# First head of a retention block: forward scan before the query sum, which goes in halves

## The reference

```
q = rotary(q); k = rotary(k) * Dh**-0.5           # x*cos + swapped(x)*sin
scores = (q_chunk @ k_chunk.T) * decay_in         # inside a chunk
inner  = scores @ v
chunk_kv = (k * zeta).T @ v                       # state that a chunk adds
state  = chunk_decay * state + chunk_kv           # scan over the 16 chunks
cross  = (q * xi) @ state_before_the_chunk
y = inner + cross     # once forward, once backward, summed, then normed and gated
```

## Time and profile before

| | us |
|---|---|
| median of 3 runs | 2922.72 |
| lowest and highest | 2922.49, 2923.69 |
| the profiled execution | 2928.47 |
| its span, first to last instruction | 2926.4 |
| TensorE busy | 2803.2 (96%) |
| VectorE busy | 1371.2 (47%) |
| GpSimd busy | 879.6 (30%) |
| ScalarE busy | 576.0 (20%) |

### The profile page before, as it was taken

The page is one execution under the profiler, slowest core; times in us unless marked ns, Lnnn a source line. Parts: engine busy times, 40 slices in busy tenths (PEclk is TensorE's granted clock), DMA queues, the critical chain, the costliest instruction groups (busy, mean ns, idle before and its releaser), DMA issues.

```text
span 2926.4 us, 37167 instructions
## 1 busy us (share of the span) xinstructions
PE 2803.2 (96%) x13882; PEld 2357.4 (81%) x13882; DVE 1371.2 (47%) x1527; ACT 576.0 (20%) x1060; POOL 879.6 (30%) x439
## 2 busy tenths in 40 slices
PE   5899999998989999999999999999999999999998
PEld 4788888887767898888888888778988888888887
DVE  4593939486875333522414234433345224152343
ACT  5221212213544222100001001232221000010012
POOL 1242423344962000333333333220003333333331
PEclk8999999999999999999999999999999999999999
DMA  4133333326853222111111113132221111111111
GB/s 159 47 116 122 105 118 118 122 99 226 257 187 115 94 83 76 51 43 50 46 47 50 46 48 108 58 122 94 87 72 51 43 50 50 43 50 50 43 50 72
DMA packets 289754, 253.99 MB, mean 87 GB/s; under 512 B 8016, under 2 KB 253960, under 8 KB 283400
## 3 DMA queue, kind: packets, MB, share of 16 engines
q1 hardware_dynamic: 266320, 203.45, 22.3%
q10 hardware_dynamic: 23352, 49.39, 4.7%
HBM read 196.71 MB, written 56.10 MB: 86 GB/s over the span
## 4 chain that ended last, share of the span: by engine, by line
PE 81%; DVE 11%; issue 3%; DMA 2%; ACT 2%; POOL 1%; ACTq 0%; DVEq 0%; SPq 0%; POOLq 0%
PE ps L699 23%; PE ps L694 23%; PE ps L695 23%; DVE acc L1685 6%; PE ps L1038 2%; PE ps L1040 2%; PE ps L1039 2%; DVE st_f L1765 1%; DMA wb<-wqk_d 1%; DVE alo L1951 1%; PE ps L1000 0%; PE ps L1049 0%; PE ps L885 0%; DVE alo L1819 0%; DMA out<-rows 0%
## 5 line engine op out<-in xcount | busy, mean ns | idle before, releaser
L554 POOL TENSOR_SCALAR whi<-wraw 128x1024 fp32r<-128x1024 f32 x192 | 224.9, 1171 | 1920.1 <-PE ps L699 1189.9
L694 PE MATMUL ps<-ahi,whi 128*128 128x512 f32 x1376 | 543.0, 395 | 17.7 <-DVE alo L1951 11.5
L695 PE MATMUL ps<-alo,whi 128*128 128x512 f32 x1376 | 538.5, 391 | 0.0
L556 POOL TENSOR_TENSOR wlo<-wraw,whi 128x1024 fp32r<-128x1024 f32 x192 | 522.8, 2723 | 16.0
L694 PE MATMUL ps<-bhi,whi 128*128 128x512 f32 x1024 | 399.4, 390 | 2.3 <-DVE blo L1872 2.3
L695 PE MATMUL ps<-blo,whi 128*128 128x512 f32 x1024 | 398.4, 389 | 0.0
L1685 DVE SCALAR_TENSOR_TENSOR acc<-upad,taps,acc 128x2048 f32<-128x2048 f32 x120 | 347.8, 2898 | 15.7 <-DVE acc L1682 0.6
L699 PE MATMUL ps<-ahi,wlo 128*128 128x512 f32 x1376 | 340.1, 389 | 0.0
L694 PE MATMUL ps<-xhi,whi 128*128 128x512 f32 x768 | 305.8, 398 | 20.9 <-DVE xlo L1607 11.0
L694 PEld LDWEIGHTS ps<-ahi,whi 128*128 128x128 f32 x1376 | 259.9, 189 | 78.6 <-DVE alo L1951 14.9
L1523 ACT ACTIVATE ahi<-z 128x512 f32 x128 | 80.9, 632 | 1140.9 <-DVE z L1948 1140.9
(11 more groups left out here) (260 smaller groups left out, 3668.8 us busy)
## 6 DMA issues: line engine op xcount, KB each, us to landing
wraw<-in_w_ff SPq DMA_DIRECT2D x128, 512.0 KB, 3.7
proj_d<-st ACTq DMA_DIRECT2D x64, 256.0 KB, 2.5
wraw<-in_w_in SPq DMA_DIRECT2D x24, 512.0 KB, 4.5
xt<-in_x SPq DMA_DIRECT2D x16, 512.0 KB, 6.4
wraw<-in_w_xkv SPq DMA_DIRECT2D x16, 512.0 KB, 5.2
vwo_d<-pst ACTq DMA_DIRECT2D x16, 512.0 KB, 3.6
wqk_d<-pst ACTq DMA_DIRECT2D x16, 512.0 KB, 3.6
wraw<-in_w_out SPq DMA_DIRECT2D x16, 512.0 KB, 4.7
```

Source lines behind the costliest of these rows:

```text
L554: pool.tensor_scalar(whi[:, slot, :, :], wraw[:, slot, :, :], 1.0, 0.0, ALU.mult, ALU.add).then_inc(w_hi, 1)
L556: pool.tensor_tensor(wlo[:, slot, :, :], wraw[:, slot, :, :], whi[:, slot, :, :], ALU.subtract).then_inc(w_ready, 1)
L694: nc.tensor.matmul(o, whi[:, slot, k, :], hi(k), start=(k == order[0]), stop=False)
L695: nc.tensor.matmul(o, whi[:, slot, k, :], lo(k), start=False, stop=False)
```

## The change

In the first head alone, VectorE runs the forward scan right behind the straight query, and the query sum behind the scan. The sum is made in two halves of 1024 tokens, the later half first, each with a signal on a new semaphore `q_rot_up`; the old one, `q_rot`, is raised when both are done. TensorE's scores wait per quarter for the half that they read. GpSimd's decayed queries of the first head are made in eight instructions of 512 tokens in place of two of 2048, quarter by quarter in the order in which `retained` reads them, and `retained` waits for its own quarter (`decays_done`). The later heads keep their instructions; their waits on `p_qf` are renumbered, since the first head now raises it eight times.

```diff
--- before.py
+++ after.py
@@ -234,6 +234,11 @@
         pre_st = [sem("pre_st0"), sem("pre_st1")]

         G0 = 4
+
+        def decays_done(h, j=3):
+
+            return 2 * j + 2 if h == 0 else 8 + 2 * h
+
         DEC_LIN = 10 + HEADS
         DEC_EXP = 2 + 4 * HEADS

@@ -274,7 +279,7 @@
         dec_in, iot, dec_dve, dec_act = (sem(n) for n in ("dec_in", "iot", "dec_dve", "dec_act"))
         l_sin, l_cos, dpos, dlin, zero_st = sem("l_sin"), sem("l_cos"), sem("dpos"), sem("dlin"), sem("zero_st")
         p_qs, p_ks, p_qc, p_kc, p_qf = sem("p_qs"), sem("p_ks"), sem("p_qc"), sem("p_kc"), sem("p_qf")
-        r_q, r_k, q_rot, k_rot = sem("r_q"), sem("r_k"), sem("q_rotd"), sem("k_rotd")
+        r_q, r_k, q_rot, k_rot, q_rot_up = sem("r_q"), sem("r_k"), sem("q_rotd"), sem("k_rotd"), sem("q_rot_up")
         kt_mm, vt_mm, kt_ev, vt_ev = sem("kt_mm"), sem("vt_mm"), sem("kt_ev"), sem("vt_ev")
         v2, v_sum, v_cen = sem("v2"), sem("v_sum"), sem("v_cen")
         kvf_mm, kvb_mm, f_scan, b_scan = sem("kvf_mm"), sem("kvb_mm"), sem("f_scan"), sem("b_scan")
@@ -610,14 +615,20 @@
                 pool.tensor_tensor(qb_[:, :], qb_[:, :], cos_t[:, :], ALU.mult).then_inc(p_qc, 1)

             def decayed_q(h):
-                pool.wait_ge(q_rot, h + 1)
+                if h:
+                    pool.wait_ge(q_rot, h + 1)
                 pool.wait_ge(dec_act, DEC_EXP + 2 * h + 2)
                 if h:
                     pool.wait_ge(y_mm, 4 * h)
-                for dst, xi in ((q_f, xi_f), (q_b, xi_b)):
-                    pool.tensor_tensor(dst[:, :].rearrange("p (c q) -> p c q", q=P),
-                                       q_rot_b[:, :].rearrange("p (c q) -> p c q", q=P),
-                                       xi[:, bass.ds(h, 1), :].to_broadcast([P, CH, P]), ALU.mult).then_inc(p_qf, 1)
+                for part in DOWN if h == 0 else (None,):
+                    at = slice(0, S) if part is None else slice(part * NC, (part + 1) * NC)
+                    chunks = (at.stop - at.start) // P
+                    for dst, xi in ((q_f, xi_f), (q_b, xi_b)):
+                        if part is not None:
+                            pool.wait_ge(q_rot_up, 1 if part >= 2 else 2)
+                        pool.tensor_tensor(dst[:, at].rearrange("p (c q) -> p c q", q=P),
+                                           q_rot_b[:, at].rearrange("p (c q) -> p c q", q=P),
+                                           xi[:, bass.ds(h, 1), :].to_broadcast([P, chunks, P]), ALU.mult).then_inc(p_qf, 1)

             def gated(h):
                 for j, i in enumerate(TURNS[h]):
@@ -877,9 +888,12 @@
                     last.then_inc(kvb_mm, 1)

             def scores_in(h):
-                pe.wait_ge(q_rot, h + 1)
+                if h:
+                    pe.wait_ge(q_rot, h + 1)
                 pe.wait_ge(f_scan, 15 * h + 15)
                 for i in DOWN:
+                    if h == 0:
+                        pe.wait_ge(q_rot_up, 1 if i >= 2 else 2)
                     for c in range(4):
                         cc = 4 * i + c
                         last = pe.matmul(ps[:, i, c * P:(c + 1) * P], k_rot_b[:, cc * P:(cc + 1) * P],
@@ -889,7 +903,7 @@
             def retained(h, j):

                 i = DOWN[j]
-                pe.wait_ge(p_qf, 2 * h + 2)
+                pe.wait_ge(p_qf, decays_done(h, j))
                 pe.wait_ge(s_ev, 4 * h + j + 1)
                 pe.wait_ge(b_scan, 15 * h + min(4 * j + 4, 15))
                 for c in range(4):
@@ -1742,15 +1756,23 @@
                 dve.wait_ge(p_ks, h + 1)
                 dve.tensor_tensor(k_rot_b[:, :], kb_[:, :], ksb[:, :], ALU.add).then_inc(k_rot, 1)

+            def straight_q0():
+                dve.wait_ge(l_q, 16)
+                dve.wait_ge(l_cos, 16)
+                dve.tensor_tensor(qb_[:, :], qb_[:, :], cos_t[:, :], ALU.mult).then_inc(r_q, 1)
+
+            def rotate_q0():
+                dve.wait_ge(r_q, 1)
+                dve.wait_ge(p_qs, 1)
+                for half in range(2):
+                    at = slice((1 - half) * HALF, (2 - half) * HALF)
+                    dve.tensor_tensor(q_rot_b[:, at], qb_[:, at], qsb[:, at], ALU.add).then_inc(q_rot_up, 1)
+                dve.wait_ge(q_rot_up, 2)
+                dve.sem_inc(q_rot, 1)
+
             def rotate_q(h):
-                if h == 0:
-                    dve.wait_ge(l_q, 16)
-                    dve.wait_ge(l_cos, 16)
-                    dve.tensor_tensor(qb_[:, :], qb_[:, :], cos_t[:, :], ALU.mult).then_inc(r_q, 1)
-                    dve.wait_ge(r_q, 1)
-                else:
-                    dve.wait_ge(p_qc, h)
-                    dve.wait_ge(p_qf, 2 * h)
+                dve.wait_ge(p_qc, h)
+                dve.wait_ge(p_qf, decays_done(h - 1))
                 dve.wait_ge(p_qs, h + 1)
                 dve.tensor_tensor(q_rot_b[:, :], qb_[:, :], qsb[:, :], ALU.add).then_inc(q_rot, 1)

@@ -1821,13 +1843,15 @@
             rotate_k(0)
             dve.memset(st_f[:, 0, :], 0.0).then_inc(zero_st, 1)
             dve.memset(st_b[:, CH - 1, :], 0.0).then_inc(zero_st, 1)
-            rotate_q(0)
+            straight_q0()
             dve.wait_ge(dec_act, DEC_EXP)
             dve.wait_ge(zero_st, 2)

             for h in range(HEADS):
                 last = h + 1 == HEADS
                 forward_scan(h)
+                if h == 0:
+                    rotate_q0()
                 for j in range(4):
                     backward_scan(h, j)
                     masked_scores(h, j)
```

## The result

The changed kernel takes 2927.58 us (median of 20 runs, 2925.58 to 2934.32), beside 2923.2 us for the kernel before in the same rounds (20 runs). The ratio is 1.0017, with a 95% interval of 1.0010 to 1.0024: some 5 us slower, at the edge of what was called no change (5.8 us). In later rounds the ratio was 1.0009 (0.9999 to 1.0018), some 2.6 us, so the size of the loss is known only roughly. The profiled execution had a span of 2926.0 us and took 2927.95 us, less than the one of before, because its first phase happened to end 3.4 us earlier. So a whole span tells nothing here, and one distance is used from now on, the *head measure*: from the start of the first head's swapped query on GpSimd to the start of head 1's forward scan on VectorE. It is 766.59 - 717.81 = 48.78 us before.

What follows compares the result with a forecast made beforehand. TensorE holds 81% of the chain, but the first head's end hangs on GpSimd's list through `k_rot`. Delay +1.9 and clock +1.5 make +3.4 us: 2922.72 + 3.4 = 2926.1 us, range 2921.5 to 2929.

Steps and rivals of the forecast that it cites:

- Where the end hangs: End of the first head: `k_rot` of head 1, behind GpSimd's list, comes last, some 0.55 us later than TensorE's path.
- The query sum later: First head, VectorE: the query sum, now behind the scan, is ready later and delays GpSimd by 1.0 us.
- The quarters: First head, GpSimd: eight decay instructions in place of two long ones cost 0.9 to 1.0 us more.
- the lock: VectorE and GpSimd share ports, held by whoever starts first; without it the first decay quarter would start 1.1 us earlier.
- The clock: Tail before head 1's scan: TensorE's clock falls in an 8.8 us pause, costing 0.7 to 2.2 us, taken as 1.5.
- The sum: Whole kernel: +1.9 us of delay and +1.5 us of clock make +3.4 us; head 1's scan near 770.
- TensorE's path decides: Handover to head 1: the tail starts when `retained` ends, 8.5 us earlier, giving 2914.2 us; rival, 5%.
- `k_rot` gets ahead of `q_in`: Handover to head 1: VectorE has the port first, `k_rot` ends 2.3 us early, 2920.4 to 2922 us; rival, 8%.
- A low clock through the next scores: Head 1's states and scores: the clock is not back when they begin, about +9 us, 2932 us; rival, 5%.
- no clock cost: Tail before head 1's scan: only GpSimd's delay counts, +1.0 to +2.7 us, 2924.6 us; rival, 17%.
- the change does what it says: First head: scores start near 724.7, 6.0 us earlier; the rival, no start before 730, gives +1 to +2 us, 3%.

Runs made afterwards that it cites:

- e4: The changed kernel, with GpSimd starting head 1's straight query only when head 1's `k_rot` is done; ratio 1.0005 (0.9995 to 1.0014).
- e6: The changed kernel with e4's wait and head 1's straight key moved from GpSimd to VectorE; 2922.45 us, ratio 0.9988 (0.9979 to 0.9997).
- e8: The changed kernel with 72 unused identity turns on TensorE between the first head's last `retained` and head 1's key turns; ratio 1.0009 (0.9998 to 1.0021).
- e7: e6 with the wait for the next head's `k_rot` in each of the first three heads; 2921.47 us, ratio 0.9988 (0.9978 to 0.9998).
- e9: The kernel before, with only e4's wait, put into each of the first three heads; ratio 0.9997 (0.9988 to 1.0006).
- e3: The changed kernel with 56 unused identity turns on TensorE, in the same place as the 72 of e8; ratio 1.0011 (1.0001 to 1.0022).

## Why the prediction was right, and where its terms were off

- **Where the end hangs.** `k_rot` of head 1, behind GpSimd's list, was named as the last wait; the new chain says the same, e4 and e6 move the handover through it, and the second profile of the kernel before keeps its measure while TensorE is 0.5 us earlier.
- **The query sum later: 1.0 us forecast, 0.3 measured** against the swapped query in this profile. The mis-sized step is the start of the scan: it was worked out from chunk states at the low clock (5.45 us), and they ran at the full one (3.81). Which clock they get differs from one execution to the next (3.81 to 5.99 us for the same 32 records in the 14 profiles): in e8, where they took 5.55, `k_rot` is 1.84 later than before, the forecast's 1.9.
- **The quarters: 0.9 to 1.0 forecast, 0.7 measured.** From the end of the sum (721.64) to `k_in` (731.33) it is 9.69 us; before, 9.02. The first quarter stood 0.9 us for the second half of the sum, as forecast from the lock.
- **The clock: 1.5 forecast, 2.5 measured.** It was to be back 5.2 us after work was taken up; it took 8.9, with one pause of 1.46 us in the work between the key turns. That the pause is the reason is not shown. So most of `conv_vars` ran low: 5.52 us for 3.79, and the second eight key turns 1.97 for 1.14.
- **The sum: +3.4 forecast, +3.46 on the head measure.** Two terms were off by 1 us each, one each way, so the close agreement is luck; the mechanism is what was right. The scan of head 1 was forecast near 770 and came at 766.64, since the first phase ended 3.4 us earlier. The times give 5 (2.9 to 7.0) in the first rounds and 2.6 (-0.3 to 5.3) in the later ones.
- **What was missed.** The `k_rot` of later heads that stands through two GpSimd products. It gave up to 2 us in profiles of versions with the quarters or the late sum. That it explains the difference between 3.5 and 5 us is not shown: a timed run leaves no rows.
- **The rivals.** That TensorE's path decides would have given a gain; it fell. That `k_rot` gets ahead of `q_in` never happened in a first head without a wait. A low clock through the next scores didn't occur: it was back at 755.9, 17 us ahead of those scores. That there would be no clock cost, the likeliest rival with 17%, is ruled out by the stretches and by e8. And the change does what it says: the scores start 6.25 us behind the swapped query.

## What to carry to other kernels

When an engine is given a head start, look for what it will wait for at the end of it: a lead that ends in one long pause in front of serial work can cost the clock of exactly that work (here 8.38 us of pause and 2.5 us of tail). Where the chain of waits names one engine, check whether another arrives within the same microsecond, by what the engine in between did just before. Of two changes that each cost little, the pair can cost more than the sum; run both halves alone.

## What the runs showed of the hardware

- A VectorE sum of two SBUF tensors that waits behind a GpSimd product does not always go next: a second GpSimd instruction went ahead of it in 5 of 14 profiles (7.22 to 9.71 us for a sum of 2.29), always where it had begun to wait during the first of two products that follow without a pause. In e7 and e9, where GpSimd waits for the sum in each head, it took 2.28 to 2.76. What decides between 5.2 and 8.7 us is open.
- The clock fell in the tail after 56 turns, when a pause of 2.33 us and 1.09 us of work lay behind them, and held after 72, with a pause of 0.57, the same work and a pause of 2.33 (e3, e8). In e4 it fell inside a pause of 4.18 us.
